# Where VectorE adds its modulation products, and when three short chunks leave their banks

## The reference

```python
mod = c_act @ w_ada[l] + b_ada[l]
shift1, scale1, gate1, shift2, scale2, gate2 = jnp.split(mod, 6, axis=-1)
hdn = modulate(rmsnorm(x, norm1_g[l]), shift1, scale1)
q_lat, c_kv, k_pe, sb_qkv, mb_qkv, gates = jnp.split(hdn @ w_in[l], SPLIT_POINTS, axis=-1)
q = to_heads(rmsnorm(q_lat, q_norm_g[l]) @ w_uq[l], N_HEADS_MLA)
kv = to_heads(rmsnorm(c_kv, kv_norm_g[l]) @ w_ukv[l], N_HEADS_MLA)
...   # three attentions: softmax, stick-breaking, block-sparse
merged = (g_a * (o_mla @ w_o_mla[l]) + g_b * (o_sb @ w_o_sb[l]) + g_c * (o_mb @ w_o_moba[l]))
x = x + gate1[:, None, :] * (merged @ w_out[l])
hdn = modulate(rmsnorm(x, norm2_g[l]), shift2, scale2)
x = x + gate2[:, None, :] * (jnp.square(jax.nn.relu(hdn @ w_ff1[l])) @ w_ff2[l])
```

## Time and profile before

| | us |
|---|---|
| median of three runs | 2700.0 |
| the three runs | 2693.2, 2700.0, 2700.31 |
| span of the profiled execution | 2689.1 |
| TensorE busy | 2582.1 (96%) |
| VectorE busy | 2103.0 (78%) |
| ScalarE busy | 1580.2 (59%) |
| additions L2192, busy in 40 to 360 us | 31.59 |

### The profile page before, as it was taken

How to read it: one execution, slowest core, us unless ns; L and a number is a source line. 1 busy time by engine, 2 the same in 40 slices (tenths; PEclk the granted TensorE clock), 3 DMA queues, 4 the chain that set the end, 5 groups by cost and what they waited for, 6 DMA issues and landing times.

```text
span 2689.1 us, 39700 instructions
## 1 busy us (share of the span) xinstructions
PE 2582.1 (96%) x13172; PEld 2103.2 (78%) x13172; DVE 2103.0 (78%) x2445; ACT 1580.2 (59%) x2048; POOL 21.5 (1%) x39
## 2 busy tenths in 40 slices
PE   7999899999999999999999988999999999999997
PEld 5777788877777898878997766787788878787885
DVE  6776777787767656766457776998999999999998
ACT  3555444456544454344444454777777777777776
POOL 0000000000000000000000000000000000000000
PEclk8999999999999999999999998999999999999999
DMA  8766568755654765555564505999999999999995
GB/s 309 227 208 183 180 213 272 255 198 193 203 160 162 232 217 183 177 172 152 181 218 141 160 7 194 336 364 326 360 353 352 343 351 363 334 353 350 366 355 206
DMA packets 190563, 666.35 MB, mean 248 GB/s; under 512 B 22881, under 2 KB 30689, under 8 KB 189777
## 3 DMA queue, kind: packets, MB, share of 16 engines
q1 hardware_dynamic: 186512, 647.66, 69.5%
q0 software_dynamic: 3904, 16.76, 1.9%
HBM read 663.29 MB, written 1.05 MB: 247 GB/s over the span
## 4 chain that ended last, share of the span: by engine, by line
PE 84%; DVE 8%; DVEq 3%; ACT 2%; DMA 1%; issue 1%; SPq 0%; ACTq 0%
PE ps L511 41%; PE ps L517 20%; PE ps L936 7%; PE ps L943 3%; PE ps L536 3%; DVE wlo L2168 2%; PE ps L618 1%; PE ps L544 1%; ACT whi L1518 1%; DVE mod_sum L2192 1%; DVEq L2666 1%; PE ps L1378 1%; DMA proj<-in_w_ada 1%; DMA ada_raw<-in_w_ada 1%; DVE xl L2251 1%
## 5 line engine op out<-in xcount | busy, mean ns | idle before, releaser
L2168 DVE TENSOR_TENSOR wlo<-raw,whi 128x1024 fp32r<-128x1024 f32 x674 | 820.3, 1224 | 372.9 <-ACT whi L1518 364.9
L1518 ACT ACTIVATE whi<-raw 128x1024 fp32r<-128x1024 f32 x674 | 710.8, 1060 | 618.8 <-PE ps L517 445.2
L511 PE MATMUL ps<-whi,xh 128*128 128x512 f32 (+2 forms) x1152 | 460.8, 401 | 3.4 <-ACT proj L1558 3.4
L511 PE MATMUL ps<-whi,xl 128*128 128x512 f32 (+2 forms) x1152 | 448.4, 390 | 0.0
L517 PE MATMUL ps<-wlo,xh 128*128 128x512 f32 (+2 forms) x1152 | 327.4, 390 | 0.0
L511 PEld LDWEIGHTS ps<-whi,xh 128*128 128x128 f32 x1152 | 218.5, 190 | 52.4 <-ACT proj L1558 4.2
L517 PEld LDWEIGHTS ps<-wlo,xh 128*128 128x128 f32 x1152 | 216.0, 190 | 47.7
L511 PEld LDWEIGHTS ps<-whi,xl 128*128 128x128 f32 x1152 | 218.8, 190 | 43.6 <-issue 1.2
L511 PE MATMUL ps<-whi,yh 128*128 128x512 f32 (+2 forms) x592 | 236.0, 402 | 6.5 <-DVEq L2287 3.2
L511 PE MATMUL ps<-whi,yl 128*128 128x512 f32 (+2 forms) x592 | 226.5, 386 | 0.0
L2168 DVE TENSOR_TENSOR wlo<-spare,whi 128x1024 fp32r<-128x1024 f32 x168 | 205.3, 1225 | 20.1 <-ACT whi L1518 19.5
(11 more groups left out here) (436 smaller groups left out, 4013.9 us busy)
## 6 DMA issues: line engine op xcount, KB each, us to landing
raw<-in_moe_w_in SPq DMA_DIRECT2D x227, 512.0 KB, 5.1
spare<-in_moe_w_in SPq DMA_DIRECT2D x165, 512.0 KB, 5.4
mod_b<-in_moe_w_out SPq DMA_DIRECT2D x165, 512.0 KB, 5.4
raw<-in_w_ff SPq DMA_DIRECT2D x120, 512.0 KB, 4.5
raw<-in_w_in SPq DMA_DIRECT2D x96, 512.0 KB, 4.3
work<-in_moe_w_in SPq DMA_DIRECT2D x56, 512.0 KB, 5.2
work<-in_moe_w_out SPq DMA_DIRECT2D x56, 512.0 KB, 4.9
ada_raw<-in_w_ada SPq DMA_DIRECT2D x48, 512.0 KB, 4.5
```

The source lines that it names most:

```text
L511: e.matmul(ps[0:lhs[2], banks[t], at:at + width], part[:, k0 + j, t * P:t * P + lhs[2]], whi[:, slot, w], start=first and j == 0 and part ...
L1518: e.activation(whi[:, slot, :], src, ACT.Copy).then_inc(split_hi, 1)
L2168: e.tensor_tensor(wlo[:, slot, :], src, whi[:, slot, :].bitcast(F32), ALU.subtract).then_inc(split_lo, 1)
```

## The change

Two things. First, VectorE's `split` no longer calls `add_modulation`; a new function `add_modulations` does, and `pass_units` calls it at the end of the step, behind the pending copy and the pieces. Which additions belong to which step stays the same. Second, three chunks are marked urgent: the 256-column chunk of `w_uq` and the two chunks of `w_ukv`. Their copies run at the very start of the next step, ahead of its split, on ScalarE and VectorE alike. TensorE, SyncE and GpSimd keep their programs.

```diff
@@ class Counts
-        self.weave, self.pending = {}, None
+        self.weave, self.pending, self.urgent = {}, None, False
+    def evacuate_pending(self, e):
+        self.pending(e)
+        self.pending, self.urgent = None, False
@@ pass_units of ScalarE
                 for i in range(n):
+                    if c.urgent:
+                        c.evacuate_pending(e)
                     split(e, LEAD)
@@ side_chunk of ScalarE and of VectorE
-            def side_chunk(e, rows, read=None, pieces={}):
+            def side_chunk(e, rows, read=None, pieces={}, urgent=False):
...
-                c.pending = evacuate
+                c.pending, c.urgent = evacuate, urgent
@@ split of VectorE
+            def add_modulations(e, unit):
                 if not c.loops and e is not SILENT:
-                    for m in mods_after(c.n.get("unit", 0) + ahead):
+                    for m in mods_after(unit):
                         add_modulation(e, m)
@@ pass_units of VectorE
                 for i in range(n):
+                    if c.urgent:
+                        c.evacuate_pending(e)
                     split(e, LEAD)
                     c.add("unit")
                     for piece in c.passed():
                         piece(e)
                     for piece in pieces.get(first + i, ()):
                         piece(e)
+                    add_modulations(e, c.n["unit"] - 1 + LEAD)
@@ layer of ScalarE (0: first bank) and of VectorE (1: second bank)
-                side_chunk(e, Q_RANK, copy_to(q_up[:, 1, 512:768]))
+                side_chunk(e, Q_RANK, copy_to(q_up[:, 1, 512:768]), urgent=True)
                 for i in range(2):
-                    side_chunk(e, KV_RANK, copy_to(proj[:, 1, i * 512:(i + 1) * 512]))
+                    side_chunk(e, KV_RANK, copy_to(proj[:, 1, i * 512:(i + 1) * 512]), urgent=True)
```

More of the change, by code:

```diff
@@ L1907, in layer @@
                 side_chunk(e, Q_RANK, copy_to(q_up[:, 0, 0:512]))
-                side_chunk(e, Q_RANK, copy_to(q_up[:, 0, 512:768]))
+                side_chunk(e, Q_RANK, copy_to(q_up[:, 0, 512:768]), urgent=True)
                 for i in range(2):
-                    side_chunk(e, KV_RANK, copy_to(proj[:, 0, i * 512:(i + 1) * 512]))
+                    side_chunk(e, KV_RANK, copy_to(proj[:, 0, i * 512:(i + 1) * 512]), urgent=True)
                 for i in range(3):
```

## The result

The changed kernel takes 2680.7 us (median of four runs, 2677.3 to 2687.8) against 2696.7 for the kernel before beside it (four runs: the three of the table above and one more of 2693.4): a ratio of 0.9947, 95% interval [0.9931, 0.9963]. A second set of five runs gave 2685.8, ratio 0.9958 [0.9945, 0.9971]; all nine have a median of 2682.2.

A forecast was written before the change was run, and what follows sets the result against it. TensorE was taken to set the pace, with its waits on VectorE or bank copies in the attention stages winnable. 6.0 + 3.0 + 1.5 = 10.5 us off 2700.0 gave 2689.5 us; 8-in-10 range 2683 to 2698.

The forecast's parts named there:

- Short chunks: Units 30 to 32 of both layers: TensorE's waits for late bank copies go, 6.0 us won.
- Latent norm: Units 13 to 21: VectorE's drain releases ScalarE's squares 1.5 us earlier, 3.0 us won in both layers.
- Att copy: Unit 55: the copy runs ahead of the additions, its wait goes, 1.5 us won in both layers.
- Waits that stay: take_modulation at unit 68 (L2202): its waits of 4.2 us each stay, 0 won.
- A: Rival, unit 32: ScalarE's copy is what it waits for; 8.7 us won, 2691.3 us; chance 12%.
- B: Rival, latent chain: gives nothing, ScalarE or a raw tile sets its start; 7.5 us won, 2692.5 us; chance 13%.
- C: Rival, the layers: TensorE's freed time comes back as other waits before the layer ends; 2700 us; chance 12%.
- D: Rival, the layers: moved additions delay splits, making the kernel 30.6 us slower, 2730.6 us; chance 8%.

The follow-up runs named there:

- e2: Changed kernel with VectorE's additions back behind the split, ahead of the step's pieces, so only the three urgent copies remain; ratio 0.9982 to the kernel before.
- e3: Changed kernel without the urgent marks, so only the additions move behind the step's pieces; ratio 0.9963 to the kernel before.
- e5: Changed kernel with ScalarE copying its halves of the three short chunks behind its split again, only VectorE copying ahead; ratio 0.9946 to the kernel before.
- e7: Kernel before with the additions behind the piece only in the step of unit 13 of each layer, no urgent copies; ratio 0.9986 to the kernel before.
- e4: Changed kernel with take_modulation at unit 68 ahead of the pending evacuation and of side_greatest; ratio 0.9919 to the kernel before.
- e10: e4 with the gated chunk pending at unit 78 of each layer also urgent on VectorE, ahead of the split; 2669.9 us, ratio 0.9900 to the kernel before.
- e9: Changed kernel with take_modulation at unit 68 ahead of side_greatest but still behind the pending evacuation; ratio 0.9940 to the kernel before.

## Why the prediction was wrong in its number and right in its steps

**The base.** The step that failed is the base: "The median of the runs is 2700.0", and "so I forecast 2700.0 - 10.5 = 2689.5". 2700.0 was the median of three runs, two of them in the upper part; one more run moved it to 2696.7, 56 later runs have a median of 2696.6, and nine tenths of them lie below 2699.3. From 2696.7 the same 10.5 us give 2686.2, and the range's lower end, worked out in the same way (13 and 4 us lower), would be 2679.7. A base taken from three runs was thus off by a third of the gain that it was to show.

Of the 8.8 us between forecast and result the base is 3.3. Another 0.7 to 1.0 is the sum, too small by the sites, and some 2 are the part of the gain at equal clock that stays open. The rest is the draw of four runs: the second set of the same kernel (2685.8) lies inside the stated range, the median of all nine (2682.2) 0.8 us below it.

**The sum.** 11.2 to 11.5 us against 10.5. *Short chunks*: 6.0 forecast, 5.7 measured; e2 and e3 add what the text didn't say, that unit 32 would be won by either part. *Latent norm*: 3.0 forecast, 3.6 measured. Two layers don't give the same: in the first the wait for yl grew to 2.11 (forecast 1.9), in the second both waits go. There I had counted the idle times, 1.5, and 1.9 came. *Att copy*: 1.5 forecast, 1.8 measured. In both, a wait that goes brings some 0.2 us more than its idle time. *Waits that stay*: L2202 has its 4.2 in both layers, as said.

**The rivals.** A is refuted by e5, at the copy that it names. B is refuted by e7 and the table. C, the return of the freed time, occurs at yl, 1.4 us, and is in the forecast; beyond that there is no new wait in the attention stages. D, slower: TensorE waits for no split after the change either. The split ahead of which additions used to stand isn't waited for, as rows 3 and 9 said.

**The rule of the Trainium skill.** "Perfetto Trace Analysis" of the Trainium skill ("Identifying the Most-Contended Engine") has the busiest engine improved. That is TensorE (305.3 of 320 us after the change), and by that rule, as the prediction reads it, VectorE's order is worth nothing. The runs say 11 us for the order of VectorE's queue, with VectorE at 240.5 of 320 us, and 22 us with e4: the trace doesn't bear the rule out here, and its list of TensorE's waits was the better guide.

**What it missed.** The 4.2 us wait was written off: "Shifting them inside their steps leaves the sum as it is: 0 won". That is right for the additions. But the trace behind the earlier trace rows has four other instructions of the same step ahead of it, and moving the waited-for one in front won 9.3 us at unit 68 in the two layers together, nearly as much as the three terms together.

## What to carry to other kernels

For each wait of the engine that sets the pace, list what stands ahead of the awaited instruction on its own engine, in its own step; every instruction there that nobody waits for can go behind it. A release (a drain or a semaphore) counts as an instruction of that list: moving the work without its release won 0.3 of 2.2 us (e10). Read whose copy was late from the ends of the rows, not from the label, and take the base from many runs before forecasting half a per cent.

## What the runs showed of the hardware

- A wait costs more than its idle time. After the change, where the second layer's qT wait was, two groups of matmuls that follow without a wait overlap in the record (the profile models a matmul's end): one group ends at 591.96 + 1.10 = 593.06, and the next starts at 592.90. So a wait that goes brings its idle time and this 0.16: removing 0.84, 0.74 and 0.82 us won 1.03, 0.94 and 1.02.

```profile
591.96 1.10 PE L522 MATMUL ps<-wlo,xh 128*128 128x512 f32 x4
592.90 1.04 PE L623 MATMUL ps<-const,proj 128*128 128x128 f32 x8
```

- The granted clock fell behind TensorE's waits of 4.2 us in both layers of the kernel before (0.83 in the 10 us from 283 and from 785) and of the changed kernel (0.66 from 277 and from 772), and not behind the wait of 0.5 in e4 (1.00). Behind the 2.6 us of e9 it fell in the first layer and not in the second. The fall of the kernel before costs some 1.2 us at unit 68 (5.1 won, less 3.7 of wait and 0.2 of overlap), the longer one of the changed kernel 1.1 and 0.8 us more.
- The mean granted clock varies from 0.980 to 0.985 between executions of one kernel, and the span is 1.8 us longer with each 0.001 less. Over the 56 runs the spans scatter by 3.0 us (standard deviation), and by 1.5 around the line through them.
